# Eight gather rows earlier, a reordered projection, and the residual as a matmul in the expert stage of a two-block transformer kernel

## The reference

```python
s = einsum('bthpc,hpnc->bthpn', qv, sub_keys)       # two times 128 scores
top_s, top_i = lax.top_k(s, 16)                     # best 16 of each half
cand_s = top_s[..., 0, :, None] + top_s[..., 1, None, :]   # 16 x 16 sums
best_s, best_j = lax.top_k(cand_s, 16)              # best 16 of 256
expert = take_along_axis(cand_i, best_j)            # row number, 0..16383
gate = softmax(best_s)
act = gelu(einsum('btd,bthkd->bthk', x, u_tab[expert]))
y = einsum('bthk,bthkd->btd', gate * act, v_tab[expert])
x = layer_norm(DN_ALPHA * x + y, ln2_g, ln2_b)
```

## Time and profile before

| what | us |
|---|---|
| median of three runs | 2890.27 (2886.15 to 2891.97) |
| the profiled execution | 2901.86 |
| its span | 2900.1 |
| TensorE, VectorE, ScalarE, GpSimd busy | 2554.9, 1995.3, 1170.8, 683.0 |
| rows issued, first layer | 1266.6 to 1895.0 |
| rows issued, second layer | 2231.7 to 2860.0 |

### The profile page before, as it was taken

How to read it: one execution, slowest core, us unless ns; L and a number is a source line. 1 busy time by engine, 2 the same in 40 slices (tenths; PEclk the granted TensorE clock), 3 DMA queues, 4 the chain that set the end, 5 groups by cost and what they waited for, 6 DMA issues and landing times. The chain is left out here.

```text
span 2900.1 us, 45569 instructions
## 1 busy us (share of the span) xinstructions
PE 2554.9 (88%) x18150; PEld 1818.6 (63%) x18150; DVE 1995.3 (69%) x4132; ACT 1170.8 (40%) x2273; POOL 683.0 (24%) x605
## 2 busy tenths in 40 slices
PE   7998887999999899999887777789999989877776
PEld 5896776778888789975443333358998555333332
DVE  5565786579998555667776777655657777777764
ACT  4245654378887544432221232234553222222222
POOL 0002110000014000024444444410001444445442
PEclk9999999999999999999999999999999999999999
DMA  7741001289998443669999999974346999999997
GB/s 308 275 157 34 4 5 33 111 317 367 374 374 302 156 147 117 247 251 422 421 409 421 421 421 421 421 281 147 112 160 240 421 421 411 421 421 421 422 421 287
DMA packets 122711, 835.37 MB, mean 288 GB/s; under 512 B 15514, under 2 KB 20540, under 8 KB 21892
## 3 DMA queue, kind: packets, MB, share of 16 engines
q0 software_dynamic: 77600, 564.43, 47.2%
q1 hardware_dynamic: 44900, 268.03, 24.4%
HBM read 831.10 MB, written 1.05 MB: 287 GB/s over the span
## 5 line engine op out<-in xcount | busy, mean ns | idle before, releaser
L3212 PE MATMUL bank<-uv_rows,z_o 128*128 128x512 f32 x872 | 426.8, 634 | 92.1 <-ACT z_o L3340 91.9
L3212 PEld LDWEIGHTS bank<-uv_rows,z_o 128*128 128x128 f32 x872 | 172.4, 202 | 323.6 <-issue 203.8
L3555 DVE CUSTOM_DVE_ANT_0 uv_rows<-uv_rows,ring 128x1024 f32<-128x1024 f32 x218 | 265.7, 1225 | 153.8 <-DMA uv_rows<-in_peer_uv,peer_index 153.8
L3092 POOL DMA_INDIRECT uv_rows<-in_peer_uv,peer_index x218 | 249.2, 1143 | 403.6 <-PE bank L3212 249.3
L1905 DVE TENSOR_TENSOR moe_halves<-ring,moe_halves 128x1024 fp32r<-128x1024 f32 x240 | 285.6, 1223 | 29.8 <-ACT moe_halves L1823 27.5
L3212 PE MATMUL bank<-query_weights,z_o 128*128 128x512 f32 x544 | 257.2, 620 | 55.1 <-ACT z_o L3340 55.1
L3334 ACT ACTIVATE peer_gelu<-peer_act 128x4 f32<-128x4 f32 (+2 forms) x134 | 27.5, 205 | 687.4 <-DVE peer_act L3555 682.6
L3212 PE MATMUL bank<-z_mg,z_o 128*128 128x512 f32 x528 | 254.7, 627 | 54.9 <-ACT z_o L3340 54.8
L3340 ACT ACTIVATE z_o<-square,peer_wts 128x128 f32<-128x128 f32 x512 | 164.4, 390 | 255.8 <-DVE peer_wts L3569 232.6
L1823 ACT ACTIVATE moe_halves<-ring 128x1024 fp32r<-128x1024 f32 x240 | 249.0, 1059 | 45.1 <-PE bank L154 42.4
L2744 DVE TENSOR_TENSOR x_weights<-ring,x_weights 128x1024 fp32r<-128x1024 f32 x116 | 140.8, 1224 | 155.8 <-ACT x_weights L2582 155.3
(11 more groups left out here) (648 smaller groups left out, 5485.3 us busy)
## 6 DMA issues: line engine op xcount, KB each, us to landing
ring<-in_moe SPq DMA_DIRECT2D x96, 1024.0 KB, 7.1
ring<-in_w_in SPq DMA_DIRECT2D x80, 1024.0 KB, 4.9
ring<-in_mod_rows SPq DMA_DIRECT2D x16, 1024.0 KB, 4.8
ring<-in_w_out SPq DMA_DIRECT2D x12, 1024.0 KB, 8.3
ring<-in_mod_w SPq DMA_DIRECT2D x8, 1024.0 KB, 10.7
ring<-in_w_branch SPq DMA_DIRECT2D x8, 1024.0 KB, 8.7
query_weights<-in_peer_wq SPq DMA_DIRECT2D x8, 1024.0 KB, 10.7
ring<-in_peer_wq SPq DMA_DIRECT2D x6, 1024.0 KB, 6.4
```

The lines of the kernel that those rows point to most:

```text
L3092: pool.indirect_dma_start(out=row(j), out_offset=None, in_=A["peer_uv"], in_offset=bass.IndirectOffsetOnAxis(ap=index[:, g, k:k + 1], axis ...
L3212: ins = pe.matmul(bank[2 * t + c][:, :], diag[:, q % 2, i, :], row(j)[:, D + c * 512:D + (c + 1) * 512], start=(j % (PH * TOPK) == 0), sto ...
L3555: dve.tensor_tensor_reduce(u, u, xtok[:, t, :], 1.0, 0.0, ALU.mult, ALU.add, acts[:, g % 2, j % TOPK:j % TOPK + 1]).then_inc(S["dots"], 1)
```

## The change

- VectorE finds the best eight of unit 0 first (`best_eight`): from the best 8 of each half, in an 8 x 8 square of sums. It hands over eight row numbers, then finds the other eight (`next_sums`, `moments_of(1)`, `next_eight`). `found` counts one more from there on.
- Rows 0 to 7 go out with the first eight numbers. Each waits for the one projection step that has read its place (`spent`), and rows 6 and 7 for the whole projection. The order of the places is changed accordingly.
- On TensorE the rest of tile 1's projection runs in one go: half of step 3 ahead of the first scores, the rest behind them. Jobs 2 and 3 follow, and job 5 moves behind the transposes of tile 1. On ScalarE `rows_out(0)` and `deviation(1)` move ahead of two query copies.
- DN_ALPHA x is added by TensorE as the first matmul into each PSUM bank (`residual`). `combine`, `totals`, `centre` and `squares` are gone; `spread_of` takes mean and variance from PSUM. A bank's last sum has its own count (`summed`), so the first bank is read while the second is being finished. SP's third load waits for `sums` 128 instead.

```diff
...
-        places = [over[:, n, :] for n in range(2)] + z[0:3] + [over[:, n, :] for n in range(2, 5)] + \
+        places = [over[:, n, :] for n in range(2, 5)] + z[0:3] + [over[:, n, :] for n in range(2)] + \
                  [wq[:, n, :] for n in range(4)] + [spare[:, :, :].rearrange("p k t -> p (k t)")]
...
+        def summed(eng, j):
+
+            if (j + 1) % (PH * TOPK) == 0:
+                eng.wait_ge(S["summed"], 2 * (j + 1) // (PH * TOPK))
+            else:
+                eng.wait_ge(S["sums"], j + 1 - j // (PH * TOPK))
...
-                            sp.wait_ge(S["combined"], 2 * TT)
+                            sp.wait_ge(S["sums"], PH * TOPK)
...
-                        pool.wait_ge(S["found"], g + 1)
-                    if j == 0:
+                        pool.wait_ge(S["found"], g + 2 if g else 1)
+                    if j == TOPK // 2:
+                        pool.wait_ge(S["found"], 2)
+                    if place[j] < 6 and use[j] == 1:
+                        pool.wait_ge(S["spent"], place[j] + (1 if place[j] < 3 else 2))
+                    if place[j] == 6 and use[j] == 1:
                         pool.wait_ge(S["proj"], 4)
                     if place[j] >= 8 and use[j] == 1:
                         n = place[j] - 8
                         pool.wait_ge(S["job"], max(JOB_AT[2 * n + 1, t] for t in range(TT)) + 1)
                     if earlier(j) is not None:
-                        pool.wait_ge(S["sums"], earlier(j) + 1)
+                        summed(pool, earlier(j))
...
-                def out_proj(t, k):
+                def out_proj(t, k, halves=range(2)):
...
-                    for c in range(2):
+                    for c in halves:
                         ins = split_product(pe, bank[2 * t + c][:, :], a, [pieces[k][:, h, wide(c)] for h in range(2)],
                                             False, k == KT - 1)
                         if k == KT - 1:
                             ins.then_inc(S["proj"], 1)
+                        elif t and c:
+                            ins.then_inc(S["spent"], 1)
...
-                out_proj(1, 3)
+                out_proj(1, 3, (0,))
                 scores(0, 0)
+                out_proj(1, 3, (1,))
+                for k in range(4, KT):
+                    out_proj(1, k)
+                turn_rows(0)
                 job(2, 0)
                 job(3, 0)
-                out_proj(1, 4)
                 scores(1, 0)
-                for k in range(5, KT):
-                    out_proj(1, k)
-                turn_rows(0)
                 job(4, 0)
-                job(5, 0)
                 pe.wait_ge(S["scores_out"], 2)
                 turn_normed(1)
+                job(5, 0)
...
+                def residual(t):
+                    pe.wait_ge(S["x_out"], 2 * t + 2)
+                    for c in range(2):
+                        pe.matmul(bank[2 * t + c][:, :], alpha[:, :], xtok[:, t, wide(c)], start=True, stop=False)
+
                 for q, (g, i, j0, size) in enumerate(groups):
                     t = g // PH
+                    if q in (0, PH * PARTS):
+                        residual(t)
                     pe.wait_ge(S["diag"], q + 1)
                     for i in range(size):
                         j = j0 + i
+                        last = (j + 1) % (PH * TOPK) == 0
                         for c in range(2):
                             ins = pe.matmul(bank[2 * t + c][:, :], diag[:, q % 2, i, :], row(j)[:, D + c * 512:D + (c + 1) * 512],
-                                            start=(j % (PH * TOPK) == 0), stop=(j % (PH * TOPK) == PH * TOPK - 1))
-                        ins.then_inc(S["sums"], 1)
+                                            start=False, stop=last)
+                            if last:
+                                ins.then_inc(S["summed"], 1)
+                            elif c:
+                                ins.then_inc(S["sums"], 1)
...
-                    act.wait_ge(S["found"], g + 1)
+                    act.wait_ge(S["found"], g + 2)
...
-                def totals(t):
...
-                def squares(t):
...
                 def root(t):
-                    act.wait_ge(S["squares"], t + 1)
-                    act.activation(spread[:, t:t + 1], spread[:, t:t + 1], ACT.Sqrt, scale=1.0 / D, bias=C.eps[2])\
-                       .then_inc(S["root"], 1)
+                    act.wait_ge(S["spread"], t + 1)
+                    act.activation(rstd[:, t:t + 1], moments[:, t, 1:2], ACT.Sqrt, bias=C.eps[2]).then_inc(S["root"], 1)
...
                 scores_out(0, 0)
+                rows_out(0)
+                deviation(1)
                 query_out(2, 0)
                 query_out(3, 0)
                 scores_out(1, 0)
-                rows_out(0)
-                deviation(1)
                 query_out(4, 0)
...
-                    if q == PH * PARTS + 6:
-                        totals(0)
                     if q == PH * PARTS + 9:
-                        squares(0)
                         root(0)
...
-                totals(1)
-                squares(1)
                 root(1)
-                act.wait_ge(S["inverse_root"], 2)
                 act.wait_ge(S["shift"], 2)
-                act.activation(y[:, 1, 512:D], y[:, 1, 512:D], ACT.Identity, scale=spread[:, 1:2], bias=shift[:, 1:2])\
+                act.activation(y[:, 1, 512:D], bank[3][:, :], ACT.Identity, scale=rstd[:, 1:2], bias=offs[:, 1:2])\
                    .then_inc(S["normed_a"], 1)
...
+                def best_eight():
+                    a, n = slice(0, 8), TOPK // 2
+                    square = [P, n, n]
+                    c3 = cand[:, 0:n * n].rearrange("p (a b) -> p a b", a=n)
+                    w3 = spot[:, 0:n * n].rearrange("p (a b) -> p a b", a=n)
+                    two = [s[:, q, :] for q in range(2)]
+                    dve.wait_ge(S["scores_out"], SCORES_AT[0, 0] + 1)
+                    for q in range(2):
+                        step(dve.max(top[:, q, a], two[q]))
+                    settle()
+                    step(dve.tensor_tensor(c3, top[:, 0, a].unsqueeze(2).broadcast_to(square),
+                                           top[:, 1, a].unsqueeze(1).broadcast_to(square), ALU.add))
+                    for q in range(2):
+                        step(dve.max_index(ti[:, q, a], top[:, q, a], two[q]))
+                    settle()
+                    step(dve.max(chosen[:, a], cand[:, 0:n * n]))
+                    step(dve.tensor_copy(tf[:, :, a], ti[:, :, a]))
+                    settle()
+                    step(dve.max_index(bi[:, a], chosen[:, a], cand[:, 0:n * n]))
+                    settle()
+                    step(dve.tensor_scalar(part[:, 0, a], bi[:, a], 3, None, ALU.logical_shift_right))
+                    step(dve.tensor_scalar(part[:, 1, a], bi[:, a], 7, None, ALU.bitwise_and))
+                    settle()
+                    step(dve.tensor_copy(pf[:, :, a], part[:, :, a]))
+                    settle()
+                    for q, w in ((0, c3), (1, w3)):
+                        step(dve.tensor_tensor(w, pf[:, q, a].unsqueeze(2).broadcast_to(square),
+                                               iota[:, a].unsqueeze(1).broadcast_to(square), ALU.is_equal))
+                    settle()
...
+                    dve.tensor_scalar(index[:, 0, a], pf[:, 0, a], offset, None, ALU.add).then_inc(S["found"], 1)
+                def next_sums():
+                    a, b = slice(0, 8), slice(8, 16)
+                    square = [P, TOPK, TOPK]
+                    c3 = cand[:, :].rearrange("p (a b) -> p a b", a=TOPK)
+                    two = [s[:, q, :] for q in range(2)]
+                    for q in range(2):
+                        step(dve.match_replace(two[q], top[:, q, a], two[q], NEG))
+                    settle()
+                    for q in range(2):
+                        step(dve.max(top[:, q, b], two[q]))
+                    settle()
+                    for q in range(2):
+                        step(dve.max_index(ti[:, q, b], top[:, q, b], two[q]))
+                    step(dve.tensor_tensor(c3, top[:, 0, :].unsqueeze(2).broadcast_to(square),
+                                           top[:, 1, :].unsqueeze(1).broadcast_to(square), ALU.add))
+                    settle()
+                    step(dve.tensor_copy(tf[:, :, b], ti[:, :, b]))
+                def next_eight():
+                    a, b, n = slice(0, 8), slice(8, 16), TOPK // 2
+                    half = [P, n, TOPK]
+                    low3 = cand[:, 0:n * TOPK].rearrange("p (a b) -> p a b", a=n)
+                    w3 = spot[:, 0:n * TOPK].rearrange("p (a b) -> p a b", a=n)
+                    step(dve.match_replace(cand[:, :], chosen[:, a], cand[:, :], NEG))
+                    settle()
+                    step(dve.max(chosen[:, b], cand[:, :]))
+                    settle()
+                    step(dve.max_index(bi[:, b], chosen[:, b], cand[:, :]))
...
```

(92 more changed lines are left out.)

7 lines of the change are left out of this document (removed).

## The result

The changed kernel takes 2875.13 us (median of seven, 2866.31 to 2880.36) against 2890.27, 15.1 us less by the medians; the ratio is 0.9942, interval 0.9929 to 0.9955, which is 13 to 21 us. Forecast were 9.1 us (2881.2, range 2873 to 2888) and, as rival 1, 16.0 us (2874.3). The profiled executions differ by more: spans of 2873.0 and 2900.1. Of these 27.1 us, 10.9 lie outside the two stages (8.8 ahead of the first, 2.2 between them), in code that is the same in both; that is how two executions of one program differ. So in all that follows **times are counted from tile 0's transposes**, the start of the stage's head (1248.40 and 2213.44 before, 1239.64 and 2195.19 after).

What follows compares the result with a forecast made beforehand. The prediction took the DMA transfer of the gathered rows to bound the stage. Heads of 2.1 and 1.4 us plus ends of 2.2 and 3.4 gave 9.1 us, so 2881.2 us, range 2873 to 2888.

Steps and rivals of the forecast that it cites:

- rival 1: Head of both layers: the slow TensorE stretch doesn't come back; 16.0 us gained, 2874.3 us, chance 0.25.
- the lead: Start of the gather: first row issued at about 1260.8 instead of 1266.64, 5.9 us earlier.
- the search: VectorE's search for the best eight row numbers ahead of the first row: 4.0 us instead of 9.14.
- The waits for the projection: GpSimd's new waits before issuing rows hold nothing up; projection ends about 1261.8, row 6 is issued about 1268.
- the slack rule: Head: an earlier first row gains only row 10's slack, 3.4 and 2.6 us per layer, less group 0's shift.
- the shift of group 0, d = +1.2: TensorE, first layer: group 0's sums at 1288.25, 1.2 us later, as jobs 2 to 4 lose 3.4 us.
- slow TensorE just behind the first row: At tile 1's transposes, both layers: about 3.4 us lost; assumed to move with the gather's start onto jobs 2 to 4.
- d = -2.2: TensorE's chain in the first layer without the slow stretch: group 0's sums at 1284.85, 2.2 us earlier.
- the other end for the start of the packets: Gather: packets start 2.9 us behind a row's issue instead of 1.8, leaving row 10 slack of 2.2 us.
- The end: Behind each layer's last sum: `turn_back` 2.5 us earlier; second layer 3.4 us with up to 0.9 from the clock.
- SP's loads set the end: End of the first layer's stage: loads keep the DMA busy until about 1926.9, leaving 2.2 us to gain.
- rivals 2 and 3: Head: 2, lead eaten, 2885 to 2888, chance 0.20; 3, TensorE becomes the bound, 2891.5, at worst 2897, chance 0.10.

Runs made afterwards that it cites:

- e5: The kernel before, unchanged, profiled in another execution; a single execution, 2895.62 us.
- e1: The kernel before with only the new end of the stage (residual matmul, statistics from PSUM, separate bank counts); 2886.63 us, ratio 0.997.
- e3: The kernel before with only the new order of places for the rows; a single execution, 2888.96 us.
- e4: The kernel before with only job 5 moved behind the transposes of tile 1; a single execution, 2898.22 us.
- e9: The changed kernel itself, measured again beside e10; 2876.55 us, ratio 0.9955 to the kernel before.
- e11: The changed kernel with 40 unused transposes (4.4 us) on TensorE ahead of residual(0); 2882.63 us, ratio 0.9972 to the kernel before.
- e12: The kernel of e1 with 40 unused transposes (4.4 us) on TensorE ahead of group 0; a single execution, 2891.57 us.
- e8: The changed kernel with group 0's gelu and diagonals ahead of two query copies and residual(0) split into TensorE's idle times; 2873.49 us, ratio 0.9931 to before.
- e2: The changed kernel with the first row waiting for all 16 numbers; 2889.29 us, ratio 0.9984 to the kernel before.
- e6: The changed kernel with TensorE's and ScalarE's order of before; 2876.46 us, ratio 0.9941 to the kernel before.
- e7: The changed kernel with ScalarE's gelu and diagonals of group 0 ahead of two query copies; 2877.33 us, ratio 0.9944 to the kernel before.
- e10: The kernel of e8 measured again beside the changed kernel (e9); 2873.04 us, ratio 0.9942 to the kernel before.

## Why the prediction was right, and where it was wrong

**Right: the bound and the lead.** The transfer sets the stage, and the first row came 6.2 us earlier (forecast 5.9), the search 3.84 us (forecast 4.0). The waits for the projection hold nothing up. The end of the gather follows the first row: over ten layers of kernels with the first row at 18.2 and no added delay (before, e5, e1, e3, e4) the last sum is at 672.3 on average (671.0 to 673.7), over four with 12.07 and the changed order (after, e9) at 667.0 (666.5 to 667.3). 5.2 of 6.2 us come through.

**Right: the slack rule.** The lead is given back as far as group 0 is late, and the place is the step from the tenth to the eleventh row. e11 and e12 show it from both sides; e8 takes most of the gap away.

**Wrong: the shift of group 0, d = +1.2.** The failing step is the one from "both layers show a slow TensorE just behind the first row" to "so it moves with the gather". Two layers of one execution are not two witnesses. The slow stretch is missing in all 13 other profiles, one of them of the unchanged kernel. The chain without it was worked out at d = -2.2 and measured, against the profiled execution, at -2.45 in the first layer and -3.22 in the second. The step made the forecast of the head 3.5 us where 9.9 were measured, and the total of 9.1 us too small against 15.1 by the medians and 16.1 in the traces. So rival 1 was what happened, for which I gave 0.25. Its reason was still not quite it: the stretch doesn't belong to the transposes but to that execution. The Trainium skill ("SBUF — State Buffer", section "Who interferes with whom") says that DMA never contends with a compute engine. The changed kernel agrees with it where the transfers start: ScalarE copies the results of jobs 2 and 3 at 1.98 and 3.77 us behind their issue, as without a transfer (1.99 and 3.78). It was the better guide than the coincidence.

**Wrong beside it, and cancelled: the slack.** 3.4 and 2.6 us were read from an execution in which group 0 was 3 us late. In the usual one row 10 is issued at 37.8 to 40.0 instead of 40.9 and 41.6, so the slack was larger, and the new order moved row 10 less (38.4 against 39.0 on average). Group 0 itself comes no earlier than usual (36.2 against 35.3 to 36.5). Where TensorE had waited for the diagonals, group 0 could run at the lower clock: in e5 it starts behind 3.40 us of idle TensorE, the granted clock is 0.56 from 1278 to 1280, and row 10 follows 3.9 us behind it, against 2.26 in the changed kernel, whose clock stays at 1.00. Slack less shift is measured against the same row 10 of the changed kernel either way, so this error drops out of rival 1's sum.

**The size of rival 1: partly luck.** It had 16.0 us, and the traces show 16.1, but term by term it is 5.6 + 4.8 forecast against 4.4 + 5.5 for the two heads, and 2.2 + 3.4 against 2.9 + 3.3 for the two ends. The last sum of one kernel moves by up to 2 us between layers and executions (before: 671.7 to 673.6), so an agreement within 0.1 us is chance. The gap costs 1.5 to 2.2 us of transfer in the changed kernel's four layers. The slack of 3.4 us would have left 0.3 us of the first layer's lead unused (6.17 less 3.4 and 2.45), and that with the other end for the start of the packets, 2.2 us, would have left 1.5. The second is nearer.

**The end.** `turn_back` comes 3.27 and 3.26 us behind the start of the last sum instead of 5.70 and 5.69, 2.4 each (forecast 2.5). The clock gave 0.9 in the second layer, in the changed kernel's both profiles, as forecast. In the first layer the prediction let SP's loads set the end, and in the changed kernel they do: the next stage begins 0.84 us behind the last packet of the three loads in both of its profiles (also in e2, e6 and e7, at 0.79 to 0.84), but 0.7 us behind the last result copy. Where that copy ends last (before, e1, e5, e10 among others) the next stage follows 0.32 us behind it. So about 0.4 us of the shorter chain is lost to the loads. This is also why the eight transposes could take 1.09 us in one execution and 1.97 in e9 while the next stage began at 673.81 and 673.82. The loads start with the last dot product, 5.2 us earlier than before (663.58 against 668.81), and from there to the next stage it is 10.2 us instead of 12.3: 2.1 us of the 2.2 that were forecast. Counted from the last sum instead, the interval varies between 6.1 and 7.4 us over the kernels with the new end.

**The rivals 2 and 3** asked for a fallen clock or a slow TensorE in the new head. Neither showed: the granted clock is 1.00 from the first transposes to 49 us behind them in both layers of the changed kernel.

**Open:** what slowed TensorE in that one execution. It hit both layers at the same distance from the first row, which would be odd for pure chance. No experiment brought it back, so none could find its cause. That it never comes with this program is not shown either: the kernel before was profiled twice.

## What to carry to other kernels

In a stage that is one long queue of transfers, as this one, look for two numbers: when the first is issued, and by how much the first *recycled* buffer's transfer beats the end of the queue. Moving the start forward eats the second; beyond it, every microsecond of the chain that frees that buffer is paid. An odd stretch in one profiled execution should be seen in a second execution before a forecast is built on it, even where it shows twice in the same trace.

## What the runs showed of the hardware

Executions of one program differ by some 10 us of span: 2864.5 to 2878.6 over seven of the changed kernel, 2893.8 and 2900.1 in two profiles of the kernel before, 2864.4 and 2876.0 in two of the kernel of e8 and e10. Of the last difference 11 us lie ahead of the first of the changed stages. One execution had a stretch of some 7 us in each layer in which TensorE's results came up to 3.4 us later than usual behind their records, at a granted clock of 1.00 until 1276 in the first layer and until 2237 in the second; the idle time of the waiting engines at the transposes is put down to "remote". Small search steps shrink with their size: 0.42 us for 256 elements, 0.29 for 128, 0.22 for 64, 0.17 for 8 or 16. The gather moves 421 to 424 GB/s in 12 us windows without a gap.
